# A hybrid transformer and linear-attention network on one core: unit norms of queries and keys on narrow columns, in two groups

## What is computed

```python
def l2norm(x):
    xf = x.astype(jnp.float32)
    return (xf * lax.rsqrt(jnp.sum(xf * xf, axis=-1, keepdims=True) + NORM_EPS)).astype(x.dtype)
```

## Time and profile before

| | |
|---|---|
| median of 3 runs | 2400.86 us (2399.29 to 2404.33) |
| the profiled execution | 2404.75 us, its span 2402.8 us |
| mean granted TensorE clock | 0.982 of full speed |
| TensorE busy | 2285.0 us, 95% of the span |
| VectorE busy | 1191.1 us, 50% |
| ScalarE busy | 1002.8 us, 42% |
| GpSimd busy | 296.8 us, 12% |
| the stage of the change | about 1491 to 1588 us of the span |

### The profile page before, as it was taken

One profiled execution on the slowest core, in us unless ns is written; L12 is line 12 of the kernel. 1 busy time (PEld: TensorE's weight loads), 2 busy tenths in 40 slices (PEclk: granted clock), 3 DMA queues, 4 the chain that ended last, 5 costly groups with the idle time before them and its releaser, 6 DMA issues.

```text
span 2402.8 us, 51648 instructions
## 1 busy us (share of the span) xinstructions
PE 2285.0 (95%) x22977; PEld 1918.7 (80%) x22977; DVE 1191.1 (50%) x2082; ACT 1002.8 (42%) x1613; POOL 296.8 (12%) x417
## 2 busy tenths in 40 slices
PE   7999999999999999999999999989999998899876
PEld 7999887889999999887889998568747787786332
DVE  5655544376655654644276655746354455421001
ACT  5344456445444444456444443643125544213111
POOL 0100000031100100000031100046213333200000
PEclk9999999999999999999999999999999999998988
DMA  8754533256655754442256652220111101267997
GB/s 267 245 202 167 168 135 105 88 190 199 212 209 181 254 202 168 164 139 101 93 183 216 216 204 74 94 73 4 41 71 37 39 25 52 72 250 299 421 420 322
DMA packets 207886, 396.60 MB, mean 165 GB/s; under 512 B 9384, under 2 KB 107357, under 8 KB 195245
## 3 DMA queue, kind: packets, MB, share of 16 engines
q1 hardware_dynamic: 205497, 388.79, 45.6%
q0 software_dynamic: 1120, 2.17, 0.3%
q10 hardware_dynamic: 1044, 2.29, 0.3%
HBM read 392.18 MB, written 1.05 MB: 164 GB/s over the span
## 4 chain that ended last, share of the span: by engine, by line
PE 85%; DMA 5%; DVE 4%; ACT 3%; issue 2%; SPq 1%; POOL 0%; ACTq 0%; DVEq 0%; POOLq 0%
PE ps L284 85%; DMA EX<-in_moe_w_up 3%; DMA RB<-in_moe_w_up 1%; SPq L535 1%; PE ps L1170 0%; DVE wl L462 0%; DVE AR L673 0%; ACT AR L2922 0%; SPq L429 0%; ACT AR L2914 0%; DVE AR L1991 0%; PE ps L557 0%; ACT AT L1224 0%; DMA VR<-in_diff_gain 0%; DVE AR L1752 0%
## 5 line engine op out<-in xcount | busy, mean ns | idle before, releaser
L462 DVE TENSOR_TENSOR wl<-RB,wh 128x2048 fp32r<-128x2048 f32 (+5 forms) x189 | 412.3, 2185 | 273.6 <-ACT wh L453 273.2
L284 PE MATMUL ps<-H,RB 128*128 128x256 f32 (+2 forms) x1728 | 452.9, 421 | 2.5 <-ACT AR L2893 1.3
L453 ACT ACTIVATE wh<-RB 128x2048 fp32r<-128x2048 f32 (+5 forms) x189 | 342.2, 1814 | 226.4 <-PE ps L284 200.4
L284 PEld LDWEIGHTS ps<-H,RB 128*128 128x128 f32 (+1 forms) x1728 | 320.3, 190 | 114.5 <-issue 76.5
L284 PE MATMUL ps<-xhf,wl 128*128 128x256 f32 x1408 | 403.3, 286 | 3.4 <-DVE xlf L702 2.9
L284 PE MATMUL ps<-xlf,wh 128*128 128x256 f32 x1408 | 399.9, 284 | 0.0
L284 PE MATMUL ps<-xhf,wh 128*128 128x256 f32 x1408 | 399.8, 284 | 0.0
L284 PE MATMUL ps<-AR 64*64 64x64 f32 (+6 forms) x8536 | 279.6, 235 | 32.0 <-issue 15.8
L284 PEld LDWEIGHTS ps<-AR 64*64 64x64 f32 (+3 forms) x8536 | 255.2, 143 | 66.6 <-issue 54.1
L284 PEld LDWEIGHTS ps<-xhf,wl 128*128 128x128 f32 x1408 | 271.6, 193 | 14.7 <-issue 9.2
L284 PEld LDWEIGHTS ps<-xlf,wh 128*128 128x128 f32 x1408 | 271.8, 193 | 0.1
(11 more groups left out here) (437 smaller groups left out, 3431.7 us busy)
## 6 DMA issues: line engine op xcount, KB each, us to landing
RB<-in_ffn_w_gu SPq DMA_DIRECT2D x88, 1024.0 KB, 7.8
RB<-in_w_in SPq DMA_DIRECT2D x23, 2048.0 KB, 8.0
RB<-in_ffn_w_down SPq DMA_DIRECT2D x16, 2048.0 KB, 7.9
RB<-in_w_gate SPq DMA_DIRECT2D x16, 2048.0 KB, 8.7
RB<-in_ada_w SPq DMA_DIRECT2D x12, 2048.0 KB, 9.8
EX<-in_moe_w_gate SPq DMA_DIRECT2D x22, 1024.0 KB, 19.5
EX<-in_moe_w_up SPq DMA_DIRECT2D x22, 1024.0 KB, 21.6
EX<-in_moe_w_down SPq DMA_DIRECT2D x11, 2048.0 KB, 24.8
```

Of the source, the lines that this page charges most:

```text
L284: return M.matmul(o, lhsT, rhs, start=start, stop=stop, skip_group_check=True)
L453: S.activation(self.pair(h)[0], of(slot_of(*key)), ACT.Copy).then_inc(*did("high", *mark))
L462: V.tensor_tensor(lo, of(slot_of(*key)), hi.bitcast(F32), ALU.subtract).then_inc(*did("low", *mark))
```

## The change

The sums become narrow. For each 128 tokens, the square of number un is loaded as weights and multiplied by 2 columns of ones, so the sum of a token's squares stands on the token's partition, in 2 equal columns. VectorE copies one of the two for each 128 tokens into L2N, which has 24 columns: 2 for each of 0 to 3, 4 for each of 4 to 7. Root and reciprocal are then taken on L2N in place, for two groups: numbers 0 to 5 in step 8 (16 columns) and 6 to 7 in step 9 (8 columns). A column is spread back over all rows by one product for each 128 tokens: the column, broadcast to 128x128, as weights, by the identity. VectorE multiplies by the result, which it reads in PSUM.

The order changes with it. SUMS says behind which conv product each narrow sum stands (two of them in steps 4 and 8), UNITS when the spread products and multiplies come: 4 and 5 in step 9, 6 and 7 in step 10, 0 to 3 in step 12, ahead of the z product and of `form_dve`. The turn of keys 5 moves from step 9 to step 10, behind the spread products; that of keys 7 stays in step 11. ScalarE squares number n - 1 in step n, not n - 2, and waits for the sum two numbers back, not the unit norm; its copy of conv product n now comes ahead of the copies of the turns, not behind them. `conv_dve` gets a step 12.

```diff
--- before.py
+++ after.py
@@ -1797,7 +1797,15 @@
             ZN, OA = area(7168, 4, 256), area(8192, 4, 256)
             PAD = [area(U0 + 520 * i, 520).rearrange("p (s n) -> p s n", s=2) for i in range(3)]
             ACC = [area(U0 + 1560 + 512 * i, 2, T) for i in range(3)]
-            VTT, L2S, L2R = area(U0 + 3100, 2, 512), area(U0 + 4200, 2, 512), area(U0 + 5300, 2, 512)
+            VTT, L2S = area(U0 + 3100, 2, 512), area(U0 + 4200, 2, 512)
+            L2N = area(U0 + 5300, 24)
+
+            def norm_at(n):
+                return slice(2 * n, 2 * n + 2) if n < 4 else slice(4 * n - 8, 4 * n - 4)
+
+            SUMS = {3: (0,), 4: (1, 2), 5: (3,), 6: (4,), 7: (5,), 8: (6, 7)}
+            NORMS = {8: (0, 6), 9: (6, 8)}
+            UNITS = {9: (4, 5), 10: (6, 7), 12: (0, 1, 2, 3)}
             GX, GA, GG, BE = (SM[:, 1076 + 32 * i:1108 + 32 * i].rearrange("p (t n) -> p t n", t=4) for i in range(4))
             ONG, ABR = area(28032, 128), area(25856, 512)
 
@@ -1820,7 +1828,7 @@
 
             def conv_pe():
                 for n in range(13):
-                    un, tk, tv = n - 3, n - 4, n - 1
+                    tv = n - 1
                     if n == 4:
                         for k in range(KD):
                             PE.wait_ge(*at("u_a", 1, k))
@@ -1854,12 +1862,22 @@
                             ins = mm(ps[:, 0:T * ns].rearrange("p (s n) -> p s n", s=ns), sv[:, k, 128 * j:128 * j + 128],
                                      uT(k, ns), k == 0, k == KD - 1)
                         ins.then_inc(*did("conv", n))
-                    if 0 <= un < 8:
-                        wd = T * streams(un)
-                        ps = bank(("sum", f"l{un}"), ("root", f"l{un}"))
+                    for un in SUMS.get(n, ()):
+                        ps = bank(("sum", f"l{un}"), ("sum_out", un))
                         PE.wait_ge(*at("squared", "l2", un))
-                        mm(ps[:, 0:wd], ones, L2S[:, un % 2, 0:wd], True, True).then_inc(*did("sum", f"l{un}"))
-                    if tk in (5, 7):
+                        for t in range(2 * streams(un)):
+                            ins = mm(ps[:, 2 * t:2 * t + 2], L2S[:, un % 2, 128 * t:128 * t + 128], ones[:, 0:2], True, True)
+                        ins.then_inc(*did("sum", f"l{un}"))
+                    for k in UNITS.get(n, ()):
+                        ps = bank(("norms", k), ("unit_k", k))
+                        PE.wait_ge(*at("rstd_k", 8 if k < 6 else 9))
+                        at_ = norm_at(k)
+                        for t in range(2 * streams(k)):
+                            ins = mm(ps[:, 128 * t:128 * t + 128], L2N[:, at_.start + t:at_.start + t + 1].broadcast_to(
+                                [128, 128]), ident, True, True)
+                        ins.then_inc(*did("norms", k))
+                    if n in (10, 11):
+                        tk = 5 if n == 10 else 7
                         PE.wait_ge(*at("unit_k", tk))
                         by_chunks("k", tk, "k_rows", [KT[:, tk - 5 + p, :] for p in range(2)])
 
@@ -1898,7 +1916,7 @@
             def conv_act():
                 AC.wait_ge(*at("pad_zero", 2))
                 for n in range(13):
-                    sq, un, tk, tv = n - 2, n - 3, n - 4, n - 1
+                    sq, tk, tv = n - 1, {10: 5, 11: 7}.get(n), n - 1
                     if n == 10:
                         sums_act()
                     if n == 12:
@@ -1917,9 +1935,16 @@
                         wd = T * streams(sq)
                         AC.wait_ge(*at("conv_silu", sq))
                         if sq >= 2:
-                            AC.wait_ge(*at("unit_k", sq - 2))
+                            AC.wait_ge(*at("sum", f"l{sq - 2}"))
                         S.activation(L2S[:, sq % 2, 0:wd], out_of(sq), ACT.Square).then_inc(*did("squared", "l2", sq))
-                    if tk in (5, 7):
+                    if n < 12:
+                        ns = streams(n)
+                        AC.wait_ge(*at("conv", n))
+                        if n >= 3:
+                            AC.wait_ge(*at("taps", n - 3))
+                        S.activation(PAD[n % 3][:, 0:ns, 2:258], ps_of("conv", n)[:, 0:T * ns].rearrange(
+                            "p (s n) -> p s n", s=ns), ACT.Copy).then_inc(*did("padded", n))
+                    if tk:
                         for half in range(2):
                             AC.wait_ge(*at("turned", "k", tk, half))
                             S.activation(KP[:, 4 * half:4 * half + 4, (tk - 5) // 2, :], heads4(ps_of("turned", "k", tk, half)),
@@ -1929,15 +1954,10 @@
                             AC.wait_ge(*at("turned", "v", tv, half))
                             S.activation(VP[:, 4 * half:4 * half + 4, (tv - 9) // 2, :], heads4(ps_of("turned", "v", tv, half)),
                                          ACT.Copy).then_inc(*did("v_rows", tv, half))
-                    if n < 12:
-                        ns = streams(n)
-                        AC.wait_ge(*at("conv", n))
-                        if n >= 3:
-                            AC.wait_ge(*at("taps", n - 3))
-                        S.activation(PAD[n % 3][:, 0:ns, 2:258], ps_of("conv", n)[:, 0:T * ns].rearrange(
-                            "p (s n) -> p s n", s=ns), ACT.Copy).then_inc(*did("padded", n))
-                    if 0 <= un < 8:
-                        root_act(f"l{un}", T * streams(un), 1.0, EPS[:, 0:1], L2R[:, un % 2, 0:T * streams(un)])
+                    if n in NORMS:
+                        cols = slice(norm_at(NORMS[n][0]).start, norm_at(NORMS[n][1] - 1).stop)
+                        AC.wait_ge(*at("sum_out", NORMS[n][1] - 1))
+                        S.activation(L2N[:, cols], L2N[:, cols], ACT.Sqrt, bias=EPS[:, 0:1]).then_inc(*did("root_k", n))
                     if n == 11:
                         for u in steps[0:2]:
                             wide_act(u)
@@ -1949,8 +1969,7 @@
                                      ACT.Silu).then_inc(*did("conv_silu", n))
 
             def conv_dve():
-                for n in range(12):
-                    un = n - 3
+                for n in range(13):
                     if n == 9:
                         gates_dve()
                     if n == 10:
@@ -1990,13 +2009,19 @@
                                 DV.wait_ge(*upto("v"))
                                 V.scalar_tensor_tensor(out=ac, in0=src, scalar=wv, in1=ac, op0=ALU.mult,
                                                        op1=ALU.add).then_inc(*(did("v") if tap < 4 else did("taps", n)))
-                    if 0 <= un < 8:
-                        rt = L2R[:, un % 2, 0:T * streams(un)]
-                        root_dve(f"l{un}", rt)
-                        DV.wait_ge(*at("rstd", f"l{un}"))
-                        DV.wait_ge(*at("conv_silu", un))
-                        V.scalar_tensor_tensor(out=out_of(un), in0=out_of(un), scalar=128.0 ** -0.5 if un < 4 else 1.0,
-                                               in1=rt, op0=ALU.mult, op1=ALU.mult).then_inc(*did("unit_k", un))
+                    for un in SUMS.get(n, ()):
+                        DV.wait_ge(*at("sum", f"l{un}"))
+                        V.tensor_copy(L2N[:, norm_at(un)], ps_of("sum", f"l{un}")[:, 0:4 * streams(un)].rearrange(
+                            "p (t n) -> p t n", n=2)[:, :, 0]).then_inc(*did("sum_out", un))
+                    if n in NORMS:
+                        cols = slice(norm_at(NORMS[n][0]).start, norm_at(NORMS[n][1] - 1).stop)
+                        DV.wait_ge(*at("root_k", n))
+                        V.reciprocal(L2N[:, cols], L2N[:, cols]).then_inc(*did("rstd_k", n))
+                    for k in UNITS.get(n, ()):
+                        DV.wait_ge(*at("norms", k))
+                        V.scalar_tensor_tensor(out=out_of(k), in0=out_of(k), scalar=128.0 ** -0.5 if k < 4 else 1.0,
+                                               in1=ps_of("norms", k)[:, 0:T * streams(k)], op0=ALU.mult,
+                                               op1=ALU.mult).then_inc(*did("unit_k", k))
                 for u in steps[0:2]:
                     form_dve(u)
 
```

## The result

The changed kernel takes 2411.01 us (median of 7 runs, 2408.05 to 2416.91) against 2400.86 of the kernel before (7 runs): a ratio of 1.0035, with an interval of 1.0025 to 1.0044. That is 8.4 us by the ratio (the medians lie 10.15 us apart), clear of the noise, some four times the 2.1 us that were forecast, and outside the range. Its profiled execution took 2414.28 us around a span of 2412.5.

What follows compares the result with a forecast made beforehand. The prediction took TensorE, busy for 95% of the span, as the bound. Spreading +5.3, sums -0.3, holes -1.1 and -1.8 gave +2.1 us, so 2400.86 became 2403.0 us, range 2398 to 2408.

Steps and rivals of the forecast that it cites:

- The work of the products: TensorE's sums and spreading: narrow sums for wide ones -0.3 us, 24 spread products +5.3 us.
- The spread products: TensorE, steps 9, 10 and 12: 24 products at 0.2225 us each, +5.3 us, bounds 5.0 and 6.0.
- Rival 4: TensorE's weight loads don't hide: 48 instructions at 0.30 us each, 2412 us, slower; chance 0.02.
- The holes: TensorE's waits ahead of the first sum product and the turn of keys 7 both close: -1.1 and -1.8 us.
- rival 5: A new wait: TensorE waits in step 10 for the reciprocal of numbers 6 and 7; 2406 us; chance 0.04.
- rival 3: VectorE was the pace: 20.4 us less of reciprocals would show nearly whole, 2382 us; chance 0.03.
- rival 1: TensorE's clock falls longer around `gates_pe` or 16-column products: 1.7 us per further fall, 2404.7 or 2406.4; chance 0.17.
- those 1.7 us alone brought no fall: Argument against longer clock falls: the 16-column products' 1.7 us brought none before; conv 5 behind them took 7.11 us.
- The fall at 2194: Late in the kernel before, the clock fell to 0.52, cited as again behind a run of four-column products.
- a shift of 2.1 us goes through whole: Behind the stage, TensorE alone then the scan make the chain, so the whole +2.1 us reaches the time.
- rival 2: TensorE's unexplained stall of 2.83 us at 1602.86 moves: gone 2398.5 us, doubled 2407.5; chance 0.10 each way.

Runs made afterwards that it cites:

- wider sums: Changed kernel with its 24 narrow sum products made 128 columns wide instead of 2, same instruction count: ratio 1.0011 to the kernel before.
- before, 64 more: Kernel before with 64 extra 32x32 by one column products at its start, 256 instructions: ratio 1.0007.
- `gates_pe` apart: Changed kernel with `gates_pe` issued in the middle of conv product 8, narrow sums kept: ratio 1.0023; the same edit in the kernel before: 1.0004.
- both edits: Changed kernel with sums 128 columns wide and `gates_pe` in the middle of conv product 8: 2407.39 us, ratio 1.0016 to the kernel before.
- the order of ScalarE alone: Kernel before with only the change's order on ScalarE (squares one step earlier, copy out and root ahead of the turns' copies), wide sums kept: ratio 1.0008.
- the second measurement: Changed kernel timed and profiled once more, unaltered, against the kernel before: ratio 1.0030.

## Why the prediction was wrong

**The work of the products was right.** With one piece on either side, the stage goes from 105.74 (before) to 108.44 (wider sums): 2.7 us. With none it goes from 104.05 (before, 64 more) to 106.74 (wider sums, `gates_pe` apart): 2.7 again. The wider sums are a little dearer than the narrow ones, by 0.1 us for 16 instructions (1.88 against 1.77). With narrow sums no profile is without falls; 111.35 less three pieces of 1.7, an estimate, is 106.25, 2.2 us above 104.05. The forecast was 2.1.

**The spread products were right.** 16 of them are worth 111.35 - 107.80 = 3.55 us, 0.222 each; the forecast had 0.2225 from the earlier trace rows. Rival 4, weight loads in the open, falls: at 0.11 + 0.19 us for each of their 32 instructions they would have been worth 9.6 us. "Part 3: Packing small matmuls — row/col tiling" of "TensorE: Matmul & The Clock Gate" in the Trainium skill has a sentence that lets loads overlap only where row groups differ; the trace disagrees with it. The same section also names loads into the background weight buffer as ones that run ahead, and with that the trace agrees as far as it goes: it doesn't show where a load is kept.

**The holes closed, and nothing waits.** The chain's 120.08 us of products pass through steps 9, 10 and 12: no wait for group 1 (rival 5), and VectorE was not the pace (rival 3).

**The failing step is the clock.** The sum held nothing for it, on the argument of rival 1: "those 1.7 us alone brought no fall". Measured: a piece costs 1.7 us of stage, as priced (105.75 - 104.05 in the kernel before, 108.44 - 106.74 with both edits), and the changed kernel has three pieces where the one before has one. Four profiles of the kernel before, with 0 to 40 more products at its start, have one each, the fifth, with 64, has none; all six of kernels with narrow sums and `gates_pe` in its place have three. The growth of the stage, 5.7 us, splits into 2.7 from the kernel before to the wider sums, with one piece in both, and 3.0 from there to the changed kernel, with two pieces more. It is rival 1 with two further falls, to which I gave the smaller part of 0.17. (The fall at 2194 that it cites didn't follow a run of four-column products but lay inside one, which started at 2189.43 and lasted 9.04 us in the kernel before.)

**What brings the falls.** In the changed kernel it is the narrow sums: the wider ones keep their number and order and lift only the columns, three pieces become one, and the ratio goes from 1.0030 and 1.0035 to 1.0011, 4.6 to 5.8 us. With `gates_pe` apart on both sides two pieces become none, and 1.0023 becomes 1.0016, which the intervals don't separate. But narrow sums aren't needed for it. What the argument missed is that the earlier trace rows show narrow work set off by holes and wide sums: 16-column products behind a conv product, `gates_pe` behind a wide sum. With the order of ScalarE alone, both holes gone and a new wait in front of the 16-column products, two more pieces came without a single narrow sum. So the gain of 2.9 us for the holes was booked in full where that kernel's stage shows it given back, through the clock and a new wait. Why that order has more falls than the kernel before is not shown.

**What stays open.** 8.4 us less the stage's 5.7 is 2.7; in the second measurement 7.2 less 5.6 is 1.6. So a second step failed, "a shift of 2.1 us goes through whole": the part behind the stage grew as well. From the second mark to the end of the span the two profiles of the kernel before have 814.0 and 809.7 us, those of the changed kernel 817.8 and 814.4. Two things in the traces bear on it:

- The late stall of rival 2 did not vanish or double: 2.83 us at 1602.86 became 1.61 at 1610.04, and other pauses moved behind it. All rows called issue behind the stage sum to 30.9 and 29.6 us in the kernel before, and to 34.1 and 34.2 in the changed one.
- Slow clock behind the stage is no longer but shorter: 74.4 and 70.2 us before, 70.7 and 56.3 in the changed kernel. So it can't be what is missing.

A straight fit over the 18 profiles, an estimate, puts 1.05 us (standard error 0.22) on each us of pauses behind the stage and 0.25 (0.06) on each us of slow clock there. By it the changed kernel's two profiles should be 4.1 us longer for the pauses and 2.2 us shorter for the clock, 1.9 in all. That would fit 1.6 to 2.7. What isn't shown is that the surplus of instructions brings these pauses in every execution. 160 more in the kernel before gave 2.4 us at an interval of 0 to 4.8, 256 gave 1.7, and the changed kernel at 256 came out 2 to 3 us below itself at 160, which the intervals don't settle. Leaving out 16 spread products was worth nothing at a surplus of 96 and 3.8 us at 160, which would fit an effect of some 3 us; but 24 more in the kernel before, the same surplus of 96, cost nothing, though its one profile has 34.7 us of pauses. The time beyond the stage stays open.

## What to carry to other kernels

Where TensorE sets the pace, price a trade of columns for instructions in two steps: first the instructions from start to next start, which held here within 0.6 us, and then the clock, by looking at what other narrow products the new ones will stand beside once the holes close. Here the same instructions with 128 columns instead of 2 made the stage 3.0 us shorter, and moving `gates_pe` away from them took another 1.7 off the stage in one of two profiles, though not off the measured time. A difference of 0.1% or less in a kernel of this length should have its surplus of instructions held equal before it is put down to the edit: small products that do nothing gave up to 1.0010 here.

## What the hardware did that was not expected

- The clock fell while TensorE was busy for all of the stretch: 3.4, 6.8 or 10.2 us at 0.50, beside 2.6 to 6.1 us of products with 2 to 16 columns. Sums of 128 columns with the same weights, 1.88 us for 16 instructions instead of 1.77, left 3.4 us of it.
- The falls differ from execution to execution of one program: conv 5 took 8.81 us in one profile of the changed kernel and 7.11 in the other, and the slow clock in the stage was 10.2 us in both.
- A four-column product pays for a fall itself: the 64 took 3.27 us at full clock, 3.90, 4.39 or 5.25 with a fall reaching into them.
- VectorE's reciprocal follows its columns, with some 0.15 us on top (an estimate from these four): 3.35 us for 512 and 1.75 for 256, 0.24 for 16 and 0.20 for 8 in the changed kernel's VectorE timeline:

```profile
1546.08 0.24 DVE L2019 RECIPROCAL AR<-AR 128x16 f32<-128x16 f32 x1
...
1561.11 0.20 DVE L2019 RECIPROCAL AR<-AR 128x8 f32<-128x8 f32 x1
```
